# Tile 1's eight softmax exponentials in two sets of four, among the first expert rows

## The reference

```python
proj = rms_norm(h) @ w_in
attn = sliding_window_attention(q, k, v, ...)     # 8 heads of 64, window 128, sink logit, meta tokens visible
ssm  = s5_ssm(u, ...)
h = h + concat(rms_norm(attn), rms_norm(ssm)) @ w_out
h = h + peer_ffn(rms_norm(h), ...)
```

## Time and profile before

| | |
|---|---|
| median of 3 runs | 1209.04 us (1203.22 to 1209.99) |
| the profiled execution, own time | 1208.79 us |
| its span, first to last instruction | 1207.5 us |
| PE, DVE, ACT, POOL busy | 976.7, 734.5, 522.3, 300.5 us |
| mean granted clock of TensorE | 0.890 |
| read from memory | 393.38 MB, 327 GB/s over the span |
| table loads on ACT, L1557 and L1466 | 53 and 48, 1283 ns each |

### The profile page before, as it was taken

The page is one execution under the profiler, slowest core; times in us unless marked ns, Lnnn a source line. Parts: engine busy times, 40 slices in busy tenths (PEclk is TensorE's granted clock), DMA queues, the critical chain, the costliest instruction groups (busy, mean ns, idle before and its releaser), DMA issues.

```text
span 1207.5 us, 14207 instructions
## 1 busy us (share of the span) xinstructions
PE 976.7 (81%) x4768; PEld 427.3 (35%) x4768; DVE 734.5 (61%) x2007; ACT 522.3 (43%) x1399; POOL 300.5 (25%) x297
## 2 busy tenths in 40 slices
PE   5988987776777667956798877899797798899998
PEld 4655542222222222321222332223341444454564
DVE  5864665689998574557746666756656433242354
ACT  5331249734434533434645563555684213211332
POOL 0000123344334234334332323344234000000000
PEclk9998997697877889887899988899797798999999
DMA  8032898899999999999999999999999754436630
GB/s 310 34 149 79 336 402 329 289 408 414 386 379 384 424 421 425 422 422 421 419 425 425 425 421 360 425 423 418 423 401 383 308 219 174 183 148 278 240 147 18
DMA packets 51737, 395.36 MB, mean 327 GB/s; under 512 B 5536, under 2 KB 10400, under 8 KB 11472
## 3 DMA queue, kind: packets, MB, share of 16 engines
q0 software_dynamic: 37536, 270.91, 55.2%
q1 hardware_dynamic: 13552, 122.83, 25.3%
q10 hardware_dynamic: 576, 0.72, 0.2%
HBM read 393.38 MB, written 1.05 MB: 327 GB/s over the span
## 4 chain that ended last, share of the span: by engine, by line
PE 44%; DMA 20%; DVE 18%; ACT 12%; issue 3%; POOL 1%; SPq 0%; DVEq 0%; ACTq 0%; POOLq 0%
DMA expert_rows<-in_peer_uv,peer_idx 18%; PE bank L1827 16%; PE bank L1488 8%; DVE expert_rows L1428 7%; PE bank L1157 4%; ACT L1557 3%; ACT L1466 2%; PE bank L2100 2%; PE bank L2059 2%; DMA x_res<-in_x 2%; DVE r L973 2%; PE bank L706 1%; ACT peer_diag L1473 1%; ACT peer_dots L1467 1%; PE bank L1734 1%
## 5 line engine op out<-in xcount | busy, mean ns | idle before, releaser
L1488 PE MATMUL bank<-expert_rows,peer_diag 64*64 64x512 f32 x2048 | 328.2, 729 | 151.5 <-ACT peer_diag L1473 149.9
L1503 POOL DMA_INDIRECT expert_rows<-in_peer_uv,peer_idx x256 | 288.3, 1126 | 527.8 <-PE bank L1488 480.7
L1428 DVE CUSTOM_DVE_ANT_0 expert_rows<-expert_rows,HN 128x1024 f32<-128x1024 f32 x256 | 309.8, 1222 | 132.7 <-DMA expert_rows<-in_peer_uv,peer_idx 130.3
L1827 PE MATMUL bank<-w_ring,b_xt 128*128 128x512 f32 (+1 forms) x576 | 292.6, 629 | 9.3 <-ACT b_sq L1858 4.4
L1466 ACT ACTIVATE peer_dots<-peer_dots 128x1 f32<-128x1 f32 x256 | 51.6, 201 | 320.9 <-DVE peer_dots L1428 314.8
L1488 PEld LDWEIGHTS bank<-expert_rows,peer_diag 64*64 64x64 f32 x2048 | 62.2, 150 | 343.7 <-ACT peer_diag L1473 274.0
L1827 PEld LDWEIGHTS bank<-w_ring,b_xt 128*128 128x128 f32 x576 | 101.9, 199 | 143.1 <-issue 135.3
L1473 ACT ACTIVATE peer_diag<-peer_eyes,peer_dots 128x64 f32<-128x64 f32 x256 | 89.0, 348 | 13.5 <-PE bank L1488 5.1
L1467 ACT ACTIVATE peer_dots<-peer_dots,peer_ex 128x1 f32<-128x1 f32 x256 | 75.4, 295 | 8.3
L1557 ACT ACT_TABLE_LOAD x53 | 68.0, 1283 | 16.0 <-DMA cols<-in_cols 5.6
L1466 ACT ACT_TABLE_LOAD x48 | 61.6, 1283 | 4.3 <-DVE peer_dots L1428 3.4
(11 more groups left out here) (405 smaller groups left out, 1175.8 us busy)
## 6 DMA issues: line engine op xcount, KB each, us to landing
w_ring<-in_w_in_e SPq DMA_DIRECT2D x16, 2048.0 KB
w_ring<-in_w_in_o SPq DMA_DIRECT2D x14, 2048.0 KB
w_ring<-in_w_query SPq DMA_DIRECT2D x8, 2048.0 KB
w_ring<-in_w_out SPq DMA_DIRECT2D x4, 2048.0 KB
w_ring<-in_w_out_e SPq DMA_DIRECT2D x4, 2048.0 KB
w_ring<-in_w_out_o SPq DMA_DIRECT2D x4, 2048.0 KB
w_ring<-in_w_in SPq DMA_DIRECT2D x2, 2048.0 KB
expert_rows<-in_peer_uv,peer_idx POOLq DMA_INDIRECT x256
```

Source lines behind the costliest of these rows:

```text
L1428: t.dve.tensor_tensor_reduce(u, u, t.HN[:, it // PH, :], 1.0, 0.0, ALU.mult, ALU.add, self.dots[:, it, k:k + 1]).then_inc(*self.dotted.add())
L1488: ins = t.pe.matmul(t.PS[2 * T + r][HALF * c:HALF * (c + 1), :], self.diag[tokens, d % self.RD, :], self.slot(n)[tokens, D + c * 512:D + ( ...
L1503: t.pool.indirect_dma_start(self.slot(n), None, t.dram["peer_uv"], bass.IndirectOffsetOnAxis(ap=self.idx[:, it, k:k + 1], axis=0)).then_in ...
L1827: ins = t.pe.matmul(pa[:, 0:n], L.xt[:, k, :], t.w.at(i, k, 0, n), start=k == 0, stop=k == KT - 1)
```

## The change

For T = 1 the places for scores go from R = 3 to R = 6. The exponentials no longer come one in a step: step 5 (row 11) has those of heads 0 to 3, step 9 (row 15) those of heads 4 to 7, each set in a row on ACT, and the sink's exponential follows the second set in the same step. `turns`, `places` and `mixes` go to 6, 7 and 8, so attention has 17 steps on PE and ACT where it had 14, and everything that follows in `rest` begins three rows later: mixing in row 26, the SSM in 33, closing in 86, the query in 93. `as1` doubles, and `mT` and `zs` are allocated ahead of it, so that it lies over `zT`, `sg`, `mT` and the first part of `zs`, where `pm1` ends too. Tile 0 keeps its order.

```diff
--- before.py
+++ after.py
@@ -545,14 +545,15 @@
     width = n_k * P + META
     tiles, meta = [n * (P + META) for n in range(n_k)], slice(P, P + META)
     bias = t.window[:, P + META:] if T == 0 else t.window[:, 0:width]
-    R = 3
+    R = (3, 6)[T]
     banks = (t.PS[0],) if T == 0 else (t.PS[4], t.PS[5])
     B = len(banks)
     s_at = lambda i, e: banks[i % B][:, e * width:(e + 1) * width]
     p_at = lambda i, e: t.as_[T][:, i % R, e * width:(e + 1) * width]
     turn_banks, out, apt = ((t.PS[2],), (t.PS[2], t.PS[6]))[T], t.PS[3], t.apt[T]
     TB = len(turn_banks)
-    sums, exps, turns, places, mixes = ((0, 1, 2, 3, 4), (1, 2, 3, 4, 5))[T]
+    sums, exps, turns, places, mixes = ((0, 1, 2, 3, 4), (1, 5, 6, 7, 8))[T]
+    at_once = {n + exps: (n,) for n in range(NU)} if T == 0 else {5: range(0, 4), 9: range(4, 8)}
 
     def pe():
         t.pe.wait_ge(*t.heads_ready[T])
@@ -666,15 +667,14 @@
                     t.act.wait_ge(*mixed.at(n - 1))
                 t.act.activation(apt[:, n % 2, :, :, :].rearrange("p e n m -> p (e n m)"),
                                  turn_banks[n % TB][:, 0:E * n_k * P], ACT.Copy).then_inc(*placed.add())
-            if exps <= i < NU + exps:
-                n = i - exps
+            for n in at_once.get(i, ()):
                 t.act.wait_ge(*least.at(n + 1))
                 logs(t)
                 for e, h in enumerate(sets[n]):
                     ins = t.act.activation(p_at(n, e), p_at(n, e), ACT.Exp, bias=t.amn[:, h:h + 1], scale=-1.0,
                                            accum_out=t.aden[:, h:h + 1])
                 ins.then_inc(*expd.add())
-            if i == NU + exps:
+            if i == (NU + exps, 9)[T]:
                 t.act.wait_ge(*sunk.at(1))
                 logs(t)
                 t.act.activation(t.adsk[:, :], t.adsk[:, :], ACT.Exp).then_inc(*sunk.add())
@@ -2624,9 +2624,9 @@
     t.uT = area.sb("uT", [P, 4, TOK])
     start = area.at
     t.zT, t.sg = (area.sb(x, [P, 4, P]) for x in ("zT", "sg"))
+    t.mT, t.zs = (area.sb(x, [P, 4, P]) for x in ("mT", "zs"))
     over = Room(t.nc, start, area.at)
-    as1, pm1 = over.sb("as1", [P, 3, SEQ + META]), over.sb("pm1", [P, PH, META])
-    t.mT, t.zs = (area.sb(x, [P, 4, P]) for x in ("mT", "zs"))
+    as1, pm1 = over.sb("as1", [P, 6, SEQ + META]), over.sb("pm1", [P, PH, META])
     t.small, t.gb = area.sb("small", [P, 15, ST]), area.sb("gb", [P, 4])
     t.last, t.state, t.st4 = area.sb("last", [P, 2, ST]), area.sb("state", [P, 2, ST]), area.sb("st4", [P, 4, ST])
     t.ssq, t.root, t.rstd = (area.sb(x, [P, 8]) for x in ("ssq", "root", "rstd"))
```

## The result

Over 20 runs each, alternating on the same chips, the kernel before took 1212.34 us and the changed one 1200.91 us; the ratio is 0.9909, with a 95% interval of 0.9893 to 0.9926: **0.9% faster**, some 11 us. Forecast were 1199.0 us and 9.8 us, counted from one execution of 1208.79 us, which lies 3.5 us under this median of 20. The profiled execution after has a span of 1198.9 us, against 1207.5 us.

The account below looks back on a forecast made before the run. No single engine bounds the whole span; in tile 1's attention a full ACT, busy with table loads, leaves DMA idle. 2.3 us (PE) plus 7.5 us (three rows) make 9.8 us: 1208.79 to 1199.0 us, range 1192 to 1210.

Parts of the forecast that it names:

- ACT and its loads: Tile 1's attention, 182 to 224 us: seven pairs of table loads go, 18.0 us of ACT; ACT no longer bounds the stage.
- PE's term, 2.3 us: Tile 1's attention: PE ends last, 38.6 us of work at clock 0.71 plus 5.7 us gaps; division 2.3 us earlier.
- The three rows, 7.5 us: After attention: three more expert rows are done at the same point of remaining work, 2.49 us each, 7.5 us.
- DMA can deliver: Up to 395 us: DMA can bring the 4.1 MB for 9.8 us, having left 7.05 and 3.9 MB unused.
- Costed at nothing: List of possible added waits and work, on DVE, masks, gather 32, first scores and shared buffers, each taken as no cost.
- The wait at tile 1's first scores: Choice in row 102: DVE may stop 0.6 us for the copy kept in row 98, costed at nothing.
- a wait much above 1 us there: Sign of being wrong: a new DVE wait at tile 1's first scores much above 1 us.
- The masks' waits: Tile 1's attention: masks of heads 6 and 7 wait for a turn one step older; taken 0, bound 6.4 us in all.
- gather 32: Gather that waits for attention's end; POOL was to wait no longer than before, costed at nothing.
- Half rate, with pauses or without: Rows 11 to 22: PE at clock 0.50; without pauses 1209.5 us, chance 0.22; with pauses 1215.2 us, chance 0.08.
- DMA as the next bound, 1192: Rival for attention: PE gets full clock, memory sets the pace, 16.7 us gained, 1192.1 us; chance 0.15.

## Why the prediction was right

**ACT and its loads: right, and shown.** The seven pairs are the cause: back in their place, the gain is gone; with all nine away, and without the order, the room or the rows, it is there. ACT's busy time was put at 24 us and is 25.79; the two sets at 5.9 and 6.1 us, and they took 5.67 (191.21 to 196.88) and 6.04.

**PE's term, 2.3 us: two sizes off that partly cancelled, and PE came last by 0.4 us only.** The meta product ended 5.4 us earlier. Between 182 and 223.20 us PE was busy 32.0 us, not 38.6, at a clock of 0.84, not 0.71. These 32.0 even hold 2.9 us of rows 6 and 7, which were left over at 182 us in both kernels and which the sum leaves out. PE idled the other 9.2 us instead of 5.7: 6.8 in the two sets and 2.4 ahead of the first, mostly for a mask on DVE, for which the sum had nothing. So 6.6 us less work and 3.5 us more idling: 3.1 us, by which 226.3 and 223.2 differ. No run tells why a PE that had more to do was granted the higher clock. As to the mechanism, PE did come last, as predicted, but by the 0.37 us that the division waited for it; in the trace with filled pauses a PE at a clock of 0.96 brings the division forward by no more than 0.5 us.

**The three rows, 7.5 us: right, but not whole.** From the division to the first dot of the SSM's first row it took 22.9 us before (228.73 to row 30 at 251.67) and 25.5 after (223.30 to row 33 at 248.76): 2.5 us went back while DVE waited 7.0 us for rows, at a DMA share of 1.00. The step that has no place for it is the one that said that DMA can deliver: it counted the bytes left over, not when they were needed. That this wait is the cause is not shown: with half-width gathers for rows 14 to 25 the same way still took 25.4 us (223.02 to 248.43). Then 5.4 - 2.5 + 7.5 = 10.4 us, which is what row 33 shows. Two misses of 3.1 and 2.5 us with opposite signs put the sum close to its mark, and that is luck. How the gain divides between an earlier division and later rows is a matter of the order: counted from row 9, the division came 10.0 us earlier with four sets and one row, 15.8 us with no loads and no row, and those kernels gained as much as the change or a little more. That three rows are worth what the sum says is borne out by the run with the later steps alone, which lost 7.9 us at the division and, within its interval of some 3 us, nothing at the end.

**Costed at nothing.** The wait at tile 1's first scores was put at 0.6 us and was 1.77. The prediction had set a wait much above 1 us there as a sign of being wrong; but nothing was lost by it that lasted (11.4 us ahead at row 102, 9.5 at row 103, 11.3 again at row 105). The masks' waits came to nothing: in the change no mask between 182 and 224 us waits for a turn. Nor does gather 32 wait for attention's end: it is issued at 232.94 us, 9.6 us after the division began.

**The rivals.** Half rate, with pauses or without: not so, the mean clock, 0.84, stayed above the 0.65 that a gain over 6 us needed. The pause did what this rival says, half rate behind the second set, but for two rows only. DMA as the next bound, 1192: not reached by the change, though its share was 0.95 and 1.00 in the first two stretches; with no loads at all DMA does fill attention (408 GB/s), and even then the ratio is 0.9886, two tenths of a per cent from the change.

## What to carry to other kernels

Where an engine is full of switches between two states, count the switches and not the work: eight exponentials of half a microsecond cost nine round trips of 2.57 us here. Grouping needs room for the operands that wait and makes everything behind it later; here the later start cost nothing that could be told, as other work ran on meanwhile, and that can be measured by idling. Stop when the full engine has come free of the bound: four sets did as well as two, and matmuls that raised the clock brought nothing that could be told.

## What the runs showed of the hardware that was not expected

Gathers for 64 of the 128 tokens, with 8 KB for each, do not take half of DMA's time: in the changed kernel DMA stayed at a share of 1.01 and 1.00 and moved 209 and 205 GB/s, where whole rows moved up to 424; in the same stretches of the kernel before, with the same gathers, it moved 137 and 131 GB/s at 0.63 and 0.59. A gather for all 128 tokens with 4 KB for each does relieve it: share 0.49 and 0.51 at 164 and 163 GB/s. The bytes are the same in both.
